# Moving transfers and steps in the tick schedule of a one-core decoder-layer kernel

## The reference

```python
h = x + W_out . concat[ Retention(RMSNorm(x)), SlidingWindowGQA_sinks(RMSNorm(x)) ]
y = FinalRMSNorm( h + PEER(RMSNorm(h)) )

# PEER, in blocks of 128 tokens
q = (xt @ peer_w_q).reshape(t, 8, 2, 128)
s = einsum('thcd,hcnd->thcn', q, peer_sub_keys)      # scores against 128 keys, twice per head
sv, si = top_k(s, 16)                                # best 16 of each half
cand = sv[..., 0, :, None] + sv[..., 1, None, :]     # 256 sums
best, sel = top_k(cand, 16)                          # best 16 of them
idx = take_along_axis(cand_idx, sel); gates = softmax(best)
h = einsum('thkd,td->thk', peer_u[idx], xt)          # 128 experts per token
a = gelu(h) * gates
out = einsum('thk,thkd->td', a, peer_v[idx])
```

## Time and profile before

| | us |
|---|---|
| median of 3 runs | 2988.2 |
| lowest and highest | 2985.72, 2996.01 |
| the profiled execution | 2987.24 |
| its span, first to last instruction | 2985.1 |
| mean granted TensorE clock | 0.864 of full speed |

### The profile page before, as it was taken

How to read it: one execution, slowest core, us unless ns; L and a number is a source line. 1 busy time by engine, 2 the same in 40 slices (tenths; PEclk the granted TensorE clock), 3 DMA queues, 4 the chain that set the end, 5 groups by cost and what they waited for, 6 DMA issues and landing times.

```text
span 2985.1 us, 33446 instructions
## 1 busy us (share of the span) xinstructions
PE 2262.5 (76%) x10572; PEld 1126.2 (38%) x10572; DVE 2079.2 (70%) x5271; ACT 1092.7 (37%) x3326; POOL 1212.0 (41%) x1068
## 2 busy tenths in 40 slices
PE   8798978577799676996787777866786568768764
PEld 6566625122466223662243222422242133414311
DVE  3576458975686556875569874797569865986975
ACT  2133433353343332432434342343534353332332
POOL 0133344444333344334444433444444444544543
PEclk9899989778899798997899788977898788977767
DMA  9899999999999999999999999999999999999998
GB/s 365 331 401 409 401 420 421 413 414 418 411 399 380 421 421 420 408 401 395 421 421 404 416 408 419 421 402 421 418 420 414 414 414 419 420 399 383 414 413 361
DMA packets 196626, 1214.40 MB, mean 407 GB/s; under 512 B 27904, under 2 KB 47176, under 8 KB 62688
## 3 DMA queue, kind: packets, MB, share of 16 engines
q0 software_dynamic: 148608, 1082.20, 88.1%
q1 hardware_dynamic: 47840, 130.07, 11.2%
HBM read 1192.48 MB, written 20.23 MB: 406 GB/s over the span
## 4 chain that ended last, share of the span: by engine, by line
DMA 31%; DVE 28%; PE 27%; issue 5%; ACT 5%; POOL 3%; DVEq 0%; SPq 0%; POOLq 0%; ACTq 0%
DMA ring<-in_peer_uv,idxg 25%; DVE ring L1858 15%; PE ps L1053 12%; PE ps L719 6%; POOL ring L643 3%; DVE columns L1704 3%; PE ps L1014 2%; PE ps L968 2%; DVE columns L1698 2%; DMA proj_scratch<-wo 2%; ACT ring L1114 2%; DMA wo<-in_xT_sample 1%; DVE columns L1710 1%; DVE columns L1767 1%; DVE columns L1770 1%
## 5 line engine op out<-in xcount | busy, mean ns | idle before, releaser
L643 POOL DMA_INDIRECT ring<-in_peer_uv,idxg x1024 | 1190.9, 1163 | 1611.3 <-PE ps L1053 1421.3
L1053 PE MATMUL ps<-ring 128*64 128x512 f32 x4096 | 1231.0, 731 | 650.1 <-ACT ring L1114 639.7
L1858 DVE SCALAR_TENSOR_TENSOR ring<-ring,xlo 128x1024 f32<-128x1024 f32 x512 | 627.4, 1225 | 377.9 <-DMA ring<-in_peer_uv,idxg 335.9
L1858 DVE SCALAR_TENSOR_TENSOR ring<-ring,xhi 128x1024 f32<-128x1024 f32 x512 | 627.2, 1225 | 311.8 <-DMA ring<-in_peer_uv,idxg 293.7
L1053 PEld LDWEIGHTS ps<-ring 128*64 128x64 f32 x4096 | 286.1, 156 | 1353.3 <-ACT ring L1114 919.7
L1336 ACT ACTIVATE small<-small 128x2 f32<-128x2 f32 x512 | 103.8, 203 | 1503.6 <-DVE ring L1858 1483.1
L1114 ACT ACTIVATE ring<-gdiag,small 128x64 f32<-128x64 f32 x1024 | 300.3, 340 | 16.8
L1014 PEld LDWEIGHTS ps<-work,wq 128*128 128x128 f32 x2304 | 273.4, 196 | 85.0 <-issue 83.6
L1114 ACT ACTIVATE gdiag<-fold,gateg 128x64 f32<-128x64 f32 x1024 | 293.0, 333 | 3.0
L1014 PE MATMUL ps<-work,wq 128*128 128x128 f32 (+1 forms) x2304 | 292.2, 280 | 1.1 <-ACT work L1114 1.1
L719 PE MATMUL ps<-wo 128*128 128x176 f32 x1680 | 271.2, 318 | 11.4 <-ACT wo L1114 5.5
(11 more groups left out here) (211 smaller groups left out, 1646.6 us busy)
## 6 DMA issues: line engine op xcount, KB each, us to landing
wo<-in_w_in SPq DMA_DIRECT2D x41, 704.0 KB
ring<-in_peer_uv,idxg POOLq DMA_INDIRECT x1024
wo<-in_w_out SPq DMA_DIRECT2D x4, 4096.0 KB, 17.5
ring<-in_w_in SPq DMA_DIRECT2D x8, 1408.0 KB, 8.2
wq<-in_w_q SPq DMA_DIRECT2D x4, 2048.0 KB, 25.2
proj_scratch<-wo SPq DMA_DIRECT2D x93, 88.0 KB
columns<-proj_scratch SPq DMA_DIRECT2D x7, 896.0 KB
h<-in_x_prompt SPq DMA_DIRECT2D x9, 512.0 KB, 8.0
```

Of the source, the lines that this page charges most:

```text
L643: nc.gpsimd.indirect_dma_start(row[r], None, A["peer_uv"], bass.IndirectOffsetOnAxis(ap=experts, axis=0)).then_inc(ld_row[r], 16)
L1053: mm = nc.tensor.matmul(acc[side * HP:(side + 1) * HP, n * 512:(n + 1) * 512], row_u[r][:, 0:HP], row_v[r][:, n * 512:(n + 1) * 512], star ...
L1858: ins = stt(row_u[r], row_u[r], 1.0, (xlo, xhi)[unit % 2][:], ALU.mult, ALU.mult, accum_out=dot[:, r:r + 1])
```

## The change

Six things are edited, all of them numbers or places in the schedule; no instruction is added or taken away.

- The load of a chunk for tiles 4 to 8 is due 4 ticks after the last piece of the chunk two before, where it was 1.
- The picks of blocks 1 to 7: the first quarter's 13 steps keep one tick each, and quarters 2 to 4 start 16 ticks apart with their steps spread over 16 ticks. Before, all quarters had 14 ticks (13 times 1.08).
- MOVES of quarters 2 to 4 go from 106, 119, 134 to 109, 125, 141.
- Fronts 2, 3, 6 and 7 begin 2, 2, 4 and 8 ticks later. The pieces of tiles 4 to 8, whose ticks hang on fronts 2 and 3, move with them by 2.
- `load_columns` goes from 12 to 14 ticks of a front.
- The samples' front, with their picks, begins at tick 9 of block 7, where it was 13, and the load of the samples' residual rows is issued inside SP's walk through the ticks, at tick 9 of block 7, where it was after its end.

```diff
--- before.py
+++ after.py
@@ -57,7 +57,7 @@
 LAST_OF = {l: max(q for q, piece in enumerate(PIECES) if piece[0] == l) for l in range(3 * LCH)}
 FIRST_TILE = LAST_OF[LCH - 1] + 1
 EARLY = LAST_OF[2 * LCH - 1] + 1
-FRONT_AT = (0, 28, 22, 24, 28, 28, 22, 16)
+FRONT_AT = (0, 28, 24, 26, 28, 28, 26, 24)
 LOWER, UPPER = range(3, 5), range(5, 10)
 AHEAD = UPPER[-1] + 1
 FILLERS = 4
@@ -128,8 +128,9 @@
 
     if b == 0:
         return FIRST_PICKS[quarter] + int(step * (FIRST_PACE if quarter else 1))
-    at, pace = (LAST_AT, 1) if b == NB else (PICK_AT, 1.08)
-    return at + PICKS_FROM + int((quarter * PICK_TICKS + step) * pace)
+    if b == NB:
+        return LAST_AT + PICKS_FROM + quarter * PICK_TICKS + step
+    return PICK_AT + PICKS_FROM + quarter * LATER_TICKS + (step * LATER_TICKS // PICK_TICKS if quarter else step)
 
 
 def hold(eng, sem, count):
@@ -443,7 +444,7 @@
                     sp.dma_start(xT_late[:, 4 * D:], A["xT_sample"]).then_inc(ld_xT, 16)
                     for l in range(l0, l0 + LCH // 2):
                         if l > l0 + 1:
-                            yield late_tick(LAST_OF[l - 2]) + 1
+                            yield late_tick(LAST_OF[l - 2]) + 4
                         load_late(l)
 
             def late_stores():
@@ -594,7 +595,7 @@
                 for b in range(1, NB):
                     yield front_at(b) - (4 if b == 1 else 9)
                     load_early_columns(b)
-                    yield front_at(b) + 12
+                    yield front_at(b) + 14
                     load_columns(b)
                     yield front_at(b) + 36
                     if b in (1, 3, 4, 5):
@@ -606,16 +607,16 @@
                 for b in range(NB - 1):
                     yield (b + 1) * TICKS + 6
                     store_y(b)
+                yield (NB - 1) * TICKS + 9
+                sp.wait_ge(st_y, 16 * NB)
+                sp.wait_ge(residual_in, NB)
+                sp.dma_start(h[0:NS, :], x_s).then_inc(ld_res, 16)
 
             parts = [late_loads(), late_stores(), sample(), y_stores(), moves(), front_loads()]
             due = [next(part_) for part_ in parts]
             for now in range(NB * TICKS):
                 for i, part_ in enumerate(parts):
                     due[i] = advance(part_, due[i], now)
-
-            sp.wait_ge(st_y, 16 * NB)
-            sp.wait_ge(residual_in, NB)
-            sp.dma_start(h[0:NS, :], x_s).then_inc(ld_res, 16)
 
             sp.wait_ge(mixs_ready, NB)
             sp.dma_start(out[2][0].rearrange("h d e -> d h e"), state[:]).then_inc(st_misc, 16)
@@ -1964,13 +1965,13 @@
                 (3, True, 17))
 SAMPLE_AT = front_at(4) + 57
 PICK_AT = 47
-PICKS_FROM, PICK_TICKS = 28, 13
-LAST_AT = 13
+PICKS_FROM, PICK_TICKS, LATER_TICKS = 28, 13, 16
+LAST_AT = 9
 FIRST_END = PICK_AT + PICKS_FROM + PICK_TICKS
 FIRST_PICKS = (PICK_AT + PICKS_FROM, FIRST_END + 9, FIRST_END + 18, FIRST_END + 27)
 FIRST_PACE = 0.7
 FIRST_MOVES = (0, 19, 28, 37)
-MOVES = (90, 106, 119, 134)
+MOVES = (90, 109, 125, 141)
 SPREAD_PAIR = 48
 
 
```

## The result

The changed kernel takes 3002.95 us (median of 20 runs, 2986.99 to 3013.7), the kernel before 2992.98 (20 runs, 2975.43 to 3005.15) in the same comparison. The forecast was 2983.0 with a range up to 2998. Two single executions of the later comparisons, one of the kernel before (6881.31 us) and one of experiment 4 (3054.82 us), lie far off the others and are in no ratio.

What follows compares the result with a forecast made beforehand. Transfers at 421 GB/s were taken as the bound, leaving 100.5 us of holes to win; -6 - 2 + 1 + 2 = -5 against 2987.2 gave 2982, or 2983 for the median, called no measurable change; range 2968 to 2998.

Steps and rivals of the forecast that it cites:

- weight loads: Tiles 4 to 8: stores issued ahead of weight loads close holes in blocks 2 and 3; 6 us won, bounds 7.6 to nothing.
- starts of blocks 1, 4, 5: First ticks of these blocks: selections now fall elsewhere, so half of their 7.7 us loss is won, 4 us.
- start of block 6, of block 2: Selections now fall on or just ahead of these starts: block 6 pays some 2 us anew, block 2 some 1.5.
- lighter pace elsewhere: Picks over 16 gathers keep VectorE at 2.38 us a tick, below the gathers' 2.49: 1.5 us won everywhere.
- picks' tail over what follows: Picks' later end overlaps the next front's mixing on VectorE, five ticks in block 1, three in blocks 5, 6: no cost.
- column loads: Block 0: two ticks' delay, 6 us more, mostly covered by the ring of gathers; 1 us lost, bounds 0 and 4.
- samples and block 7: Block 7's last picks fall on the samples' norm, then first scores are waited for: 2 lost, bounds 1 won, 5 lost.
- the 18.2 of slack: Block 2: time from a weight load's issue to TensorE's chunk start, 18.2 us, taken to cover the load's delay.
- rival 2: Weight loads behind up to five stores take 21.1 us, TensorE waits 35 us; +10, 2998.5 us; chance 0.17.
- a sign of being right: ScalarE's store waits under 20 us, block 2 ticks 24 to 31 over 380 GB/s, blocks 4, 5 starts losing under 2.
- Rival 1: Landed gathers' pile was everything: all four block starts lose nothing, both holes close; -15, 2973 us; chance 0.35.
- The pile: Landed gathers in the ring while VectorE lags under the picks, 2.2 too many, paid for at the next block start.

Runs made afterwards that it cites:

- experiment 4: Changed kernel with the samples' front back at tick 13 of block 7: 2998.94 us, ratio to before 1.0007.
- experiment 1: Kernel before with only the weight loads of tiles 4 to 8 due 4 ticks after instead of 1: 2987.63 us, ratio to before 0.9981.
- experiment 12: Changed kernel with front 2 at tick 28 instead of 24: 3000.39 us, ratio to before 1.002.
- experiment 3: Changed kernel with the column loads back at 12 ticks of a front: 3001.65 us, ratio to before 1.0015.
- experiment 2: Kernel before with only the column loads moved from 12 to 14 ticks of a front: 2999.4 us, ratio to before 1.0016.
- experiment 5: Kernel before with quarters 2 to 4 of picks over 16 gathers, MOVES and the samples' residual load moved with them: 2995.97 us, ratio 1.001.
- experiments 8 and 9: Changed kernel, column loads at 12 ticks, block 4's picks at old pace; 8 also has samples' picks 4 ticks later: 2986.47 us (8), 2993.72 us (9).
- Experiment 7: Changed kernel with the samples' picks 4 ticks later against their queries: 2998.8 us, ratio to before 1.0022.
- experiment 6: Changed kernel with the picks of block 4 alone at their old pace: 2996.06 us, ratio to before 1.0005.
- experiment 10: Changed kernel, column loads at 12, block 4's picks at old pace, front 7 at 16, samples' front at 13: 2997.36 us, ratio to before 1.0014.

## Why the prediction was wrong

By its steps, from the two profiles (holes in us):

| term | predicted (bounds) | measured |
|---|---|---|
| weight loads | -6 (-7.6 to 0) | -6.9, by luck in part; alone -9.0, and -5.7 in the time |
| starts of blocks 1, 4, 5 | -4 | -7.1 |
| start of block 6, of block 2 | +2, +1.5 | +2.2, -0.9 |
| lighter pace elsewhere | -1.5 | -1.9 (ticks 80 to 127 of blocks 1 to 6) |
| picks' tail over what follows | 0 | +8.6 in block 4, +3.3 in block 1, +1.3 in block 5 |
| column loads | +1 (0 to 4) | +12.1, some 7 of it at equal landing time; alone +12.8, and +4.8 in the time |
| samples and block 7 | +2 (-1 to +5) | +8.9, with the clock in it |

**Right.** The frame held: bytes and ceiling are the same, and every us is a hole. *Weight loads behind the stores* came out as priced alone (experiment 1), and in place (block 2 ticks 24 to 31 at 409 GB/s). The size in the changed kernel is partly luck. The three tile 4 to 8 stretches lose 6.9 us in its profile, but 6.4 to 14.7, 10.0 in the mean, over the nine profiles with the same loads and the same fronts 2 and 3, against 13.8 before. In block 2 a hole of 4.2 to 9.0 us opens in ticks 32 to 39 in all nine, behind a weight load that takes 17.5 to 22.3 us to land, against the 18.2 of slack. The slack had been taken from a load that went out earlier: at 949.52 in the changed kernel TensorE wants the load some 13 us after its issue. So rival 2 was right about the transfer and wrong about its number: TensorE's waits for chunks rose by 4.5 us, not 35. All that was named ahead as a sign of being right came true; none of it looked at blocks 0 and 4, which lost 12.1 and 8.6 us anew. Rival 1's mechanism came true at the starts of blocks 1, 4 and 5, which lose 0.6 instead of the 3.7 that I left there. (The pile worked out for it, 45.3 us at 420 GB/s less 16 gathers, is 2.1 gathers and not 2.2.) The loss at block 2's start, called a price that no order changes, was 2.3 us before, 1.4 in the changed kernel and 4.5 in experiment 12. "Slower by over 0.3%" had a chance of 0.17, all of it rival 2's. It came by two paths that no rival named.

**Wrong, first: the column loads.** The step was "The ring covers most; I take 1 lost, bounds 0 and 4". The delay was sized right: two ticks took 6 to 7 us of TensorE's room in front of the transfer (experiment 3), and 6 were worked out. The load had been waited for 2.8 us already, so it had no slack, and 2.8 + 6 = 9 us of wait were to be expected. 13.0 came, because the load also took 21.23 us to land instead of 17.04. What failed is the cover. The ring covers a wait of up to 2.8 us but at most 2 us of one of 7 or more, since the gathers are released by the very engine that stands. The upper bound should have been the whole wait, not 4. (The column load of L510 is 896 KB by the profile of experiment 2, whose row of DMA issues has a median of 21.8 us to landing, and the early one 640 KB; the section on the kernel has these two the other way round.)

**Wrong, second: the picks' tail.** The step was "they overlap for some five ticks there and three in blocks 5 and 6. I cost that at nothing". It named blocks 1, 5 and 6, where 3.3 and 1.3 us were lost in blocks 1 and 5, and did not look at what else VectorE has in block 4, the samples' mixing at its ticks 29 to 34. VectorE's work in those 16 ticks went from 33.17 to 40.26 us. The row I read for the pace, 40.76 us in 16 ticks taking 45.30, was the warning of what that costs. The priced question was how even the picks run; the unpriced one was into which ticks their end moves. It ate what the starts gave (experiment 5). That these two steps make the sign is shown by experiments 8 and 9: without them the kernel is not slower than before.

**Third: block 7.** "I take 2 lost", and the profile has 9. How much of it is the order of the steps is open, because the stretch's length goes with TensorE's clock (the last section). Experiment 7 removes VectorE's wait and leaves TensorE busy throughout; experiment 4 gives 7.5 us in the time that its profile doesn't place.

The Trainium skill, "DMA: Bandwidth & Descriptors", section "Queues, rings and completion order", was drawn on for the store behind a load, with the two queues at half the rate each. The ring order agrees: with the load behind the stores their waits are 3.4 us in the changed kernel and 0.2 in experiment 1, from 42.5. The halves, which were my reading, do not. The page of the changed kernel for 283.48 to 304.71 us, the flight of the column load; q0 are the gathers, q1 SP's transfers:

```profile
q0 software_dynamic: 861, 6.27, 70.1%
q1 hardware_dynamic: 1033, 2.66, 31.3%
```

SP's queue had 31% of the engines' time and moved 2.66 MB in 21.23 us, 125 GB/s. The numbers of packets are close, 861 and 1033, but a gather's are 7.3 KB in the mean and SP's 2.6, so turns alike in number would come out unequal in bytes; whether the engines take turns so is not shown. At that rate 704 KB more in front of a transfer are 5.8 us, not the 3.4 of my estimate, close to the longest store wait of 6.0 in the earlier trace rows, and 896 KB are 7.3.

## What to carry to other kernels

Where one resource is full, price a move by where each moved step *ends* and what else its engine has there, not by its pace; here 7.1 us more work in 16 ticks, on an engine that was busy for 33.2 of the 39.8 that the gathers need, cost 8.6. A transfer that is waited for at all has no slack: its delay goes one for one into the wait. If the waiting engine frees the buffers of the prefetch, the prefetch covers a wait of 2 or 3 us here and not one of 7. Measure the room between issue and need against the time to landing in several profiles, since here the same load took 16 or 22 us. Try the parts of such a change one by one: here one was worth 6 us, one cost about 5, one gave back its own gain, and the version with the places mended beats both kernels.

## What was not expected of the hardware

**The granted clock in block 7.** The same instructions took very different times from one profile to the next. Timeline of TensorE, the first 32 query matmuls of the samples, in the changed kernel:

```profile
2714.32 7.00 PE L1015 MATMUL ps<-work,wq 128*128 128x8 f32 x32
```

and in experiment 6, with the same code there:

```profile
2714.24 3.74 PE L1017 MATMUL ps<-work,wq 128*128 128x8 f32 x32
```

The one is nearly twice the other; the granted clock was 0.50 of full speed under the first, the level of 1.2 GHz, and 0.98 under the second, close to that of 2.4 GHz. The kernel before had 3.89. Before these matmuls TensorE had stood 5.12 us for ScalarE in both of the two shown (at 2694 and 2696). The 28 us from 2714 on, in the table by stretch, again the changed kernel and then experiment 6:

```profile
2714.00:2742.00 28.00, 28.00 (x106) 19.61 (x104) 11.16 (x29) 8.06 (x25) 6.56 (x6) 0.50 0.73 266
2714.00:2742.00 28.00, 27.42 (x167) 17.35 (x165) 20.27 (x62) 10.03 (x31) 11.06 (x10) 0.88 0.99 386
```

In the first the clock stands at the lower level throughout, TensorE is never idle and gets through 106 instructions instead of 167, and the transfers run at 266 GB/s, a hole of 10.3 us out of some 15. Over the fourteen profiles ticks 32 to 47 of block 7 took 43.8 to 46.7 us at a mean clock of 0.81 (three profiles), 46.1 to 50.6 at 0.73 to 0.75 (three), and 46.5 to 56.1 at 0.62 to 0.72 (eight); the code of the changed kernel alone spans 43.8 to 56.1, that of before 46.5 to 54.3. So a difference of under 10 us in this stretch, in one profile each, says nothing on the order of its steps. What sets the clock there wasn't tried.

**The same load, 16 or 22 us.** The column load of block 1, 896 KB, took 16.0 to 17.1 us to land in six profiles and 20.3 to 22.0 in seven, and with the same code around it both (17.11 us in experiment 10, 22.01 in experiment 3). That makes the hole in block 0 0.1 to 0.3 or 5.8 us with the load at 12 ticks, and 7.6 or some 12 at 14. If both happen among the timed executions, too, a hole of one profile is no measure of the mean; 12.8 us between two profiles stand against 4.8 (-0.6 to +10) in the time.
